# Moving two modulation slices of a two-block transformer kernel from the attention stage to the up projection

## The reference

```
mod = c @ w_ada + b_ada                    # six vectors of 1024: sh1 sc1 gt1 sh2 sc2 gt2
h = rms_norm(x, g_pre_mix) * (1 + sc1) + sh1
... attention of 3 kinds x 8 heads over proj = h @ w_in ...
x = x + gt1 * rms_norm(o @ w_out, g_post_mix)
h = rms_norm(x, g_pre_ffn) * (1 + sc2) + sh2
y = square(relu(h @ w_up)) @ w_down
x = x + gt2 * rms_norm(y, g_post_ffn)
```

## Time and profile before

| | |
|---|---|
| Median of 3 runs | 1531.42 us (1527.2 to 1542.44) |
| The profiled execution's own time | 1541.84 us |
| Its span in the profile | 1540.0 us |
| PE busy | 1444.8 us, 94% |
| DVE, ACT, POOL busy | 854.6, 743.5, 978.7 us |
| Attention stage (first scores to last values) | 144.8 to 257 us |
| Up stage, down stage | 306 to 400, 400 to 492 us |

### The profile page before, as it was taken

How to read it: one execution, slowest core, us unless ns; L and a number is a source line. 1 busy time by engine, 2 the same in 40 slices (tenths; PEclk the granted TensorE clock), 3 DMA queues, 4 the chain that set the end, 5 groups by cost and what they waited for, 6 DMA issues and landing times.

```text
span 1540.0 us, 23035 instructions
## 1 busy us (share of the span) xinstructions
PE 1444.8 (94%) x9084; PEld 1235.6 (80%) x9084; DVE 854.6 (55%) x1485; ACT 743.5 (48%) x1369; POOL 978.7 (64%) x710
## 2 busy tenths in 40 slices
PE   5798998899999899879999999999998999999998
PEld 2676656699887898559999999999997888888886
DVE  4655664445313786352589948999895333322222
ACT  2442122555545667344444455445554555555554
POOL 0564461467766453145689998877886777777775
PEclk9896896999999999989999999999999999999999
DMA  9342441444554432033544544555555666555552
GB/s 388 134 164 110 164 165 55 164 163 166 192 187 168 164 123 99 26 110 137 192 165 164 192 166 170 186 191 175 181 200 207 240 244 239 212 191 192 192 191 82
DMA packets 48588, 263.78 MB, mean 171 GB/s; under 512 B 5472, under 2 KB 14048, under 8 KB 19040
## 3 DMA queue, kind: packets, MB, share of 16 engines
q1 hardware_dynamic: 38272, 251.68, 45.3%
q10 hardware_dynamic: 10208, 10.63, 2.0%
HBM read 252.84 MB, written 9.44 MB: 170 GB/s over the span
## 4 chain that ended last, share of the span: by engine, by line
PE 62%; DVE 19%; POOL 3%; issue 1%; ACT 1%; DVEq 0%; ACTq 0%
PE bank L1385 23%; PE bank L782 21%; PE bank L748 15%; DVE arena L2608 4%; DVE hotg L2608 4%; DVE arena L2604 3%; DVE hots L2604 3%; POOL v_lo L1914 3%; PE bank L1165 1%; DVE arena L2620 1%; DVE arena L2490 1%; PE bank L763 0%; DVE hT_lo L1971 0%; PE bank L912 0%; PE bank L1331 0%
## 5 line engine op out<-in xcount | busy, mean ns | idle before, releaser
L1914 POOL TENSOR_TENSOR v_lo<-ring,v_hi 128x512 fp32r<-128x512 f32 x448 | 620.3, 1402 | 169.4 <-ACT v_hi L1814 160.4
L1906 POOL TENSOR_TENSOR v_lo<-ring,d_hi 128x512 fp32r<-128x512 f32 x213 | 291.3, 1378 | 318.4 <-ACT d_hi L1507 257.0
L1814 ACT CAST v_hi<-ring 128x512 fp32r<-128x512 f32 x512 | 315.3, 621 | 307.6 <-PE bank L1385 163.3
L748 PE MATMUL bank<-hT_hi,v_hi 128*128 128x256 f32 x1024 | 295.2, 288 | 5.3 <-POOL v_lo L1914 5.2
L748 PE MATMUL bank<-hT_lo,v_hi 128*128 128x256 f32 x1024 | 286.7, 280 | 0.0
L748 PE MATMUL bank<-hT_hi,v_lo 128*128 128x256 f32 x1024 | 286.3, 280 | 0.0
L1507 ACT CAST d_hi<-ring 128x512 fp32r<-128x512 f32 x236 | 144.3, 621 | 171.7 <-PE bank L782 150.0
L1385 PE MATMUL bank<-v_hi,mix_hi 128*128 128x512 f32 x512 | 201.9, 394 | 3.2 <-DVE mix_lo L2635 3.2
L1385 PE MATMUL bank<-v_hi,mix_lo 128*128 128x512 f32 x512 | 201.7, 394 | 0.0
L1385 PE MATMUL bank<-v_lo,mix_hi 128*128 128x512 f32 x512 | 201.7, 394 | 0.0
L748 PEld LDWEIGHTS bank<-hT_hi,v_hi 128*128 128x128 f32 x1024 | 193.0, 188 | 6.9 <-POOL v_lo L1914 6.0
(11 more groups left out here) (327 smaller groups left out, 2434.9 us busy)
## 6 DMA issues: line engine op xcount, KB each, us to landing
ring<-w_dram SPq DMA_DIRECT2D x230, 1024.0 KB, 4.8
gate_dram<-gput ACTq DMA_DIRECT2D x64, 128.0 KB, 3.2
gget<-gate_dram SPq DMA_DIRECT2D x32, 256.0 KB, 4.9
x<-x_dram SPq DMA_DIRECT2D x1, 1024.0 KB, 5.5
arena<-mem_dram ACTq DMA_DIRECT2D x1, 1024.0 KB, 11.1
out_dram<-x SPq DMA_DIRECT2D x1, 1024.0 KB, 4.0
arena<-const_dram ACTq DMA_DIRECT2D x1, 884.0 KB, 9.4
arena<-vec_dram ACTq DMA_DIRECT2D x1, 144.0 KB, 4.5
```

Source lines behind the costliest of these rows:

```text
L748: return nc.tensor.matmul(out_, lhsT, rhs, start=start, stop=stop)
L1814: nc.scalar.copy(v_hi[:, r, :], quarter(at, r)).then_inc(s_vhi, 1)
L1906: nc.gpsimd.tensor_tensor(v_lo[:, r, :], dense_quarter(d, r), d_hi[:, r, :], ALU.subtract).then_inc(s_dpl, 1)
L1914: nc.gpsimd.tensor_tensor(v_lo[:, r, :], quarter(at, r), v_hi[:, r, :], ALU.subtract).then_inc(s_plo, 1)
```

## The change

Slices 10 and 11 are no longer done by PE in the attention stage. `ROW_BLOCKS`, their 16 products, their copies by ACT and their two turns into columns go, and all units have six fillers. Their four tiles are loaded among the `up` tiles, one behind each of the groups n = 1, 2, 3, 4, and DVE weighs them after row groups 3, 5, 7, 9 of the up stage. The other `ada` tiles come in a new order, and slices 6, 7 and 9 are turned into columns in other units. PE sums slices 10 and 11 over the partitions (8 products of one column) ahead of `kg` 4 of the down stage, and spreads the second half of `gg` ahead of `kg` 6 instead of in the out stage. `s_o` is raised after each token half, and the transposes of each half wait for their own.

```
+ADA_WITH_UP = {1: ("ada", 10, 0), 2: ("ada", 10, 1), 3: ("ada", 11, 0), 4: ("ada", 11, 1)}
+
+
 def weight_tiles():
     tiles = [("ada", n + m, k) for n in range(2) for k in range(2) for m in (0, 2)]
     tiles += [("in", n, k) for n in range(5) for k in range(2)]
     tiles += [("cmp1", n, 0) for n in range(2)]
-    tiles += [("ada", n, k) for n, k in ((4, 0), (5, 0), (4, 1), (11, 0), (5, 1), (6, 0), (7, 0), (11, 1), (6, 1),
-                                         (7, 1), (8, 0), (10, 0), (9, 0), (10, 1), (8, 1), (9, 1))]
+    tiles += [("ada", n + m, k) for n in (4, 6, 8) for k in range(2) for m in range(2)]
     tiles += [("out", n, k) for n in range(2) for k in range(2)]
     tiles += [("mem_kv", 0, k) for k in range(2)]
...
-    tiles += [("up", n, k) for n in range(8) for k in range(2)]
+    for n in range(8):
+        tiles += [("up", n, k) for k in range(2)]
+        if n in ADA_WITH_UP:
+            tiles += [ADA_WITH_UP[n]]
     tiles += [("down", kg, n) for kg in range(8) for n in range(2)]
...
-ADA_ROWS = [("ada", n, k) for n in (2, 3, 11, 10) for k in range(2)]
+ADA_ROWS = [("ada", n, k) for n in (2, 3) for k in range(2)]
 ADA_POOL = [("ada", n, k) for n in range(5, 10, 2) for k in range(2)]
-ADA_VEC = [("ada", n, k) for n in (4, 6, 8) for k in range(2)]
+ADA_VEC = [("ada", n, k) for n in (4, 6, 8, 10, 11) for k in range(2)]
...
-            for m in range(4):
+            for m in range(2):
...
+    rotate(("ada", 1), [0, 1, 2, 3])
+    for m in range(2, 4):
+        rotate(("gg", m), [0, 1, 2, 3])
...
-ROW_BLOCKS = {1: (11, (0,)), 2: (11, (1,)), 3: (11, (2,)), 4: (11, (3,)), 6: (11, (4,)), 7: (11, (5,)), 8: (11, (6,)),
-              9: (11, (7,)), 12: (10, (0,)), 13: (10, (1,)), 14: (10, (2, 3)), 15: (10, (4,)), 16: (10, (5,)),
-              17: (10, (6, 7))}
-ROW_BANK = {11: 7, 10: 5}
-ROW_COPIED = {10: 11, 18: 10}
-MOD_AT = {5: 4, 6: 5, 11: 11, 13: 6, 16: 7, 19: 10, 22: 8, 24: 9}
+MOD_AT = {5: 4, 6: 5, 13: 6, 14: 7, 20: 9, 22: 8}
 WEIGH_AT = {b + (b >= 16): (("ada", 4 + 2 * ((b + 4) // 8), (b + 4) // 4 % 2), b % 4) for b in range(20)}
+ADA_AFTER = {2 * n + 1: name for n, name in ADA_WITH_UP.items()}
 FILLERS = 6
-FILLERS_ROW = 2
...
+            return ada[:, n % 4, :] if n < 8 else addb[:, n - 8, :] if n < 10 else prob[:, n - 10, :]
...
+                    if what == "oT":
+                        pe.wait_ge(s_o, tb + 1)
...
-            def ada_row_blocks(n, blocks):
-
-                if 0 in blocks:
-                    begin(("adarow", n))
-                ps = banks[ROW_BANK[n]]
-                for b in blocks:
-                    half, kk = b // 4, b % 4
-                    if kk == 0:
-                        arrived(("ada", n, half))
-                    last = mm(ps[0:1, :], vcol("c", b), km(("ada", n, half))[:, kk, :], start=(b == 0), stop=(b == 7))
-                    if b == 3:
-                        last.then_inc(s_arow, 1)
-                    if b == 7:
-                        end(last, ("adarow", n))
-                        pe.drain().then_inc(s_arow, 1)
...
-                    for _ in range(FILLERS_ROW if i + 1 in ROW_BLOCKS else FILLERS):
+                    for _ in range(FILLERS):
...
-                    if i in ROW_BLOCKS:
-                        ada_row_blocks(*ROW_BLOCKS[i])
...
-            pe.wait_ge(s_o, 1)
+            def gain_rows(m):
+
+                ps = begin(("gg", m))
+                for k in range(4):
+                    last = mm(ps[:, k * P:(k + 1) * P],
+                              gg[:, 4 * m + k:4 * m + k + 1].to_broadcast([P, P]), ident[:, :])
+                end(last, ("gg", m))
...
-                    for m in range(4):
-                        ps = begin(("gg", m))
-                        for k in range(4):
-                            last = mm(ps[:, k * P:(k + 1) * P],
-                                      gg[:, 4 * m + k:4 * m + k + 1].to_broadcast([P, P]), ident[:, :])
-                        end(last, ("gg", m))
+                    for m in range(2):
+                        gain_rows(m)
...
             for kg in range(8):
+                if kg == 4:
+                    pe.wait_ge(s_avec, len(ADA_VEC))
+                    ps = begin(("ada", 1))
+                    for n in (10, 11):
+                        for s in range(4):
+                            last = mm(ps[:, 4 * n + s:4 * n + s + 1], ada_sum(n)[:, s * P:(s + 1) * P], one)
+                    end(last, ("ada", 1))
+                if kg == 6:
+                    pe.wait_ge(s_ggf, 2)
+                    for m in range(2, 4):
+                        gain_rows(m)
...
-                    if i in ROW_COPIED:
-                        n = ROW_COPIED[i]
-                        ps = wait_full(act, ("adarow", n))
-                        free(nc.scalar.copy(ada_sum(n)[0:1, :], ps[0:1, :]), ("adarow", n))
-                        wait_read(act, ("adarow", n))
-                        nc.scalar.copy(stat[:, 152:153], one).then_inc(s_arc, 1)
...
+            high_parts(("down", 6, 0))
+            for n in range(2, 4):
+                gain_rows(n)
...
-            link(tt(gg[:, 8:16], mod[:, 40:48], vall("g_post_ffn"), ALU.mult))
...
-            nc.vector.memset(coef[:, 0:1], 0.0).then_inc(s_o, 1)
+                nc.vector.memset(stat[:, 153 + tb:154 + tb], 0.0).then_inc(s_o, 1)
...
+                if n in ADA_AFTER:
+                    weigh(ADA_AFTER[n])
+            low_parts(("down", 4, 0))
+            ps = wait_full(dve, ("ada", 1))
+            free(tt(mod[:, 40:48], ps[:, 40:48], vcol("b_ada", 40, 8), ALU.add), ("ada", 1))
+            wait_read(dve, ("ada", 1))
+            tt(gg[:, 8:16], mod[:, 40:48], vall("g_post_ffn"), ALU.mult).then_inc(s_ggf, 1)
```

More of the change, by code:

```diff
@@ L280, in attention_groups @@
             group(("S", *units[i]), i % 2)
-        if i in ROW_BLOCKS and 0 in ROW_BLOCKS[i][1]:
-            group(("adarow", ROW_BLOCKS[i][0]), ROW_BANK[ROW_BLOCKS[i][0]])
         if 1 <= i <= n:
@@ L415, in build @@
         ggb = take(2, D)
-        addb = take(4, 512)
+        addb = take(2, 512)
         block1_end = where[0]
@@ L420, in build @@
         take(D_FF // P, T)
-        assert where[0] <= block1_end - 2 * D - 4 * 512
+        assert where[0] <= block1_end - 2 * D - 2 * 512
         sbqT = take(4, T, at=common)
@@ L633, in ada_sum @@
         def ada_sum(n):
-            return ada[:, n % 4, :] if n < 8 else addb[:, n - 8, :]
+            return ada[:, n % 4, :] if n < 8 else addb[:, n - 8, :] if n < 10 else prob[:, n - 10, :]
         v_hi = nc.alloc_sbuf_tensor_at("v_hi", [P, 4, 512], F32R, offset=x_at)
@@ L862, in modulation_columns @@
                     pe.wait_ge(s_avec, ADA_VEC.index(("ada", n, 1)) + 1)
-                elif ("ada", n, 1) in ADA_POOL:
+                else:
                     pe.wait_ge(s_apool, ADA_POOL.index(("ada", n, 1)) + 1)
-                else:
-                    pe.wait_ge(s_arc, 3 + (n == 10))
                 for s in range(4):
[L868 to L872, removed]
+                    last = mm(ps[:, 384 + s:385 + s], ada_sum(n)[:, s * P:(s + 1) * P], one)
                 return last
@@ L1609, in _, with gain_rows @@
             high_parts(("out", 1, 1))
-            for n in range(4):
+            def gain_rows(n):
                 ps = wait_full(act, ("gg", n))
                 free(nc.scalar.copy(ggb[:, n // 2, (n % 2) * 512:(n % 2 + 1) * 512], ps[:, :]), ("gg", n))
+            for n in range(2):
+                gain_rows(n)
             row_squares("out", 2)
```

## The result

| | before | after |
|---|---|---|
| Median beside each other | 1532.84 us (1527.2 to 1546.8) | 1554.71 us of 6 (the five counted: 1549.91 to 1556.73) |
| Ratio after to before | | 1.0117, interval 1.0063 to 1.017 |
| Profiled execution | 1541.84 us, span 1540.0 | 1551.26 us, span 1549.4 |
| A second profile of each | 1539.31 us | 1549.13 us |

The change makes the kernel 1.2% slower, some 18 us. One execution of the changed kernel took 1637.91 us at a mean clock of 0.818 and is left out of the ratio. Their clocks fit that: 0.960 and 0.961 over the whole execution for before, 0.960 and 0.963 for after, where the five timed executions of after had 0.957 to 0.961 and 35 of before, taken beside the first experiments, a median of 0.966.

A forecast was written before the change was run, and what follows sets the result against it. PE, busy 94% of the span, was taken as the bound. Attention -12.2, tail -1.9, out stage -1.9, down stage +2.9 and up stage +14 gave +0.9 on the median 1531.42: 1532.3 us, range 1516 to 1553.

The forecast's parts named there:

- Up stage: PE waits for late `up` tile loads ahead of column groups 3, 4 and 5: +14 us, bounds 10 and 19.
- The fourth gates only the second tile of group 6: Up stage: the fourth such tile has a group's time to spare, so no wait was added for it.
- A fall of the clock in such a wait costs little more: Up stage: PE isn't the late one in the load waits, so a clock fall there adds little to the +14 us.
- Attention stage: Row blocks, two turns and a tile wait go, fillers come in, DVE limits part of the saving: -12.2 us.
- The clock there: Attention stage: fewer turns (fewer falls) and no row blocks (slower returns) cancel: 0, ends a gain of 18, loss of 34.
- clock stays up: Rival, attention stage: six fillers and fewer turns keep full clock, 18 us come back: 1514 us, half of it 1523; chance 0.14.
- Clock stays down: Rival, attention stage: without row blocks nothing brings the clock back after units 5 and 6: 1549 to 1566 us; chance 0.18.
- Tail and out stage: Behind the attention stage `s_o` is raised sooner, -1.9 us; half of `gg`'s spreading leaves the out stage, -1.9.
- down stage: Half of `gg`'s spreading returns at `kg` 6, +1.9 us; eight column products at `kg` 4, +1.0: together +2.9.
- Locked products: Rival, up stage: each of four weigh products waits out a POOL subtraction, 5.9 us a tile: 1546 us; chance 0.1.

The follow-up runs named there:

- the timed run: Changed kernel with the round of PSUM banks set back to bank 3 ahead of the second half of the memory keys: 1549.82 us, ratio 1.0067.
- The version with the tiles beside down: Changed kernel with the four tiles loaded and weighed among the down tiles (`kg` 0 to 3), banks set back: 1524.65 us, ratio 0.9932 to the kernel before.

## Why the prediction held as a whole, and where it was wrong

The forecast was 1532.3 us, +0.9. The measured ratio is +1.2%, inside the range and on the side that had 0.25. There is luck in that: two terms missed by 12 and by 3 to 6 us in the same direction, and in the profiled pairs a clock that had been put at nothing gave 10.5 us back.

**Up stage: +14 forecast, +26.4 and +24.1 measured.** This is the step that failed. Most of the mechanism was right: slot, weigh, load, split, and idle time of 4.5, 4.2 and 4.5 us ahead of groups 3, 4 and 5 where 4.5, 5.0 and 4.4 stood. By PE's starts the excess divides so, in the first pair:
- Up to the start of group 3: 42.5 us where 36.8 were the earlier trace rows, +5.7; forecast +4.5. The wait of 0.79 us for quarter 3's subtraction is most of the difference, and it was PE's own: there was no wait for the load yet to hide it.
- Two turns of the loop: 18.4 + 18.1 us where PE has 2 x 11.74, +13.0; forecast +9.4. The weighs were sized well: 4.7, 5.0 and 3.8 us where 4.0, 4.6 and 4.0 stood, and the load too. What lies between landing and weigh was not: 8.6 us in the first turn (318.90 to 327.49) and 9.5 in the second, where 7.4 stood. I had ACT's splits, relus and squares on the chain and DVE only behind the last square; in the trace DVE's subtraction of quarter 3 (1.53 us) and its four operations, two or three of them at 1.7 us beside POOL, are the chain. The row of 1.67 us lay in the earlier trace rows; I had let it count once.
- Behind the start of group 5: 43.3 us where 35.7 were (366.2 by the earlier trace rows to 401.9), +7.6; forecast 0. "The fourth gates only the second tile of group 6" is true of its load, and its weigh still blocks DVE: 4.3 us of waiting for the subtraction of quarter 3, which the prediction had called a microsecond late and hidden by the load. Here no load hid it. The other 3.3 us go with PE's work at half clock there (3.2 us behind the start of group 5 and 4.4 behind this wait).

**"A fall of the clock in such a wait costs little more."** True inside the loop, where PE's slower work only shortened its next wait; not true behind the last turn. The bounds of 10 to 19 had one fall of the clock that isn't hidden; there were four falls in all.

**The bank plan: 0 forecast, +2.7 measured,** and in the second pair 3.6 more in the stretch behind it, where 6.8 us at half clock begin in this wait; 4.9 by the timed run. The first pair's +8.2 there has 19 us more at half clock in it, 10 of them over 120 us behind this wait. The prediction has no term for what moving groups does to the banks of all later ones.

**Attention stage: -12.2 at equal clock forecast, -11.7 measured** (101.9 against 113.5 from the first scores, with 41.0 us at half in each; -10.5 from the first turn). The parts hold less well than the sum: fillers 5.6 where 7.7 stood, so by these numbers the blocks and turns brought less than was put down for them, and no run parts them. DVE's limit came near where it was expected: PE waited 0.84 and 1.28 us in units 11 and 12 where 1.5 stood; the waits are ended by ACT's exponentials, which start when DVE has the row maxima. **The clock there: 0 forecast.** Against the 41.0 us of before's two profiles it gave back up to 24 us at half, worth 10.5 us, in both profiles of after, and less in the others. That is between the forecast and the rival "clock stays up". "Clock stays down" did not happen. The step had set fewer turns against the missing blocks and had no term for the fillers themselves. The run that kept the blocks and all eight turns and only had six fillers came down from 41.0 us at half to 10.2, and its ten executions had a higher mean clock (0.974 against 0.966); so it is the fillers that lift the clock. That taking the blocks away then costs some of it (17 to 41 in place of 10.2) would fit, on one profile.

**Tail and out stage -3.8 forecast, -4.4 and -4.0 measured; down stage +2.9 forecast, +3.6 measured.** Both right as sums; PE's wait behind the attention stage fell by 1.0 us where 1.9 stood.

**"Locked products"** was a rival at 0.1, on the ground that POOL runs dry in PE's wait. Half of it held: in each weigh of the loop one or two products took 1.4 to 1.7 us and the others 0.76; in the fourth, three took 1.65. It ruled the stage only when the weigh was moved earlier.

**Open.** The timed difference is some 8 us more than that of the profiled pairs. The clock accounts for about that much: 0.006 between before's profiled executions (0.960) and its median (0.966) is 18 us at half clock over 1535 us, worth 8 us at 0.44 each. That is an estimate, since the 35 executions were taken at another time than the pair and don't tell in which stage their clock was up. So in the timed executions the changed kernel has the lower clock as a whole, though its attention stage had the higher one in the profiles. Why PE's clock falls more in some executions of the same code isn't shown. The version with the tiles beside down rests on the shorter attention stage by its stage times; the shorter attention stage alone, without the tiles in any later stage, was not run.

## What to carry to other kernels

A tile put into a queue that loads in order is paid for by whoever frees its slot: draw the loop (free, load, split, the consumer's queued work, free) and compare its period with the work of the bound engine before placing it, and place it where the consumer has nothing in its queue that the next load gates. Read also what stands behind the added work on the same engine, in each place, the last one included: an operation of 0.70 us behind 5.7 us of products stopped PE for 4.3. When groups are added or moved, write out the rotation of the banks of everything behind them and keep it in step.

## What the runs showed of the hardware

- A weigh product of DVE, or one of its operations on a row group or a quarter, took 0.69 to 0.76 us, or mostly 1.5 to 1.8 us when POOL was subtracting. With POOL's operands cut to four columns all in the up stage were short again.
- TensorE's clock fell to half in each wait of the up stage in which PE was idle for over 4 us, or up to 0.9 us behind its end, and stayed there into the work behind it. In the stage with four such waits 20.5 to 23.9 us were at half; with four of 1.8 to 4.1 us from start to start it was 13 to 14, with one of 4.3 among shorter ones 6.8, and with none 0 to 5.5. In the attention stage of after the fall came in a wait of 1.28 us that ended at 186.97, ahead of the next turn into columns, so a turn isn't the only thing before a fall:

```profile
165.00:186.70 21.70, 19.34 (x134) 1.00 0.33 122
186.70:203.80 17.10, 16.44 (x68) 0.50 0.23 94
```

The Trainium skill, page "TensorE: Matmul & The Clock Gate", section "Loop structure matters more than you think", has long waits let the engine go cold; for the up stage the trace agrees. In the attention stage 17.1 us passed at half clock, PE busy in 16.44 of them, before it came back.
